# Expert weights loaded, waited for and freed by halves in a two-layer diffusion trunk

## What is computed

```python
g_p, g_i = lax.top_k(g_prob, 1)                    # one of 4 groups
e_p, e_i = lax.top_k(softmax(e_logits), TOP_K)     # two of its 4 experts
a = jnp.einsum('td,edf->tef', t, w_gate)           # w_gate, w_up: 16 x 1024 x 512
u = jnp.einsum('td,edf->tef', t, w_up)
hid = jax.nn.silu(a) * u * gates[..., None]
y = jnp.einsum('tef,efd->td', hid, w_down)         # w_down: 16 x 512 x 1024
```

## Time and profile before

| | us |
|---|---|
| median of three runs | 1182.11 (1179.56 to 1182.42) |
| the profiled execution | 1183.99 |
| its span, first to last instruction | 1182.1 |
| TensorE busy in the span | 1107.5 (94%) |
| VectorE, ScalarE, GpSimd busy | 388.3, 235.5, 93.2 |
| chain that ended last: TensorE, DMA, VectorE | 81%, 12%, 4% |

### The profile page before, as it was taken

How to read it: one execution, slowest core, us unless ns; L and a number is a source line. 1 busy time by engine, 2 the same in 40 slices (tenths; PEclk the granted TensorE clock), 3 DMA queues, 4 the chain that set the end, 5 groups by cost and what they waited for, 6 DMA issues and landing times.

```text
span 1182.1 us, 13463 instructions
## 1 busy us (share of the span) xinstructions
PE 1107.5 (94%) x5106; PEld 533.4 (45%) x5106; DVE 388.3 (33%) x982; ACT 235.5 (20%) x521; POOL 93.2 (8%) x160
## 2 busy tenths in 40 slices
PE   5999999999999899979999989999999899889998
PEld 1455545456456633323333434455656433333334
DVE  5223143443553611111111355553746211111113
ACT  2411201433224200000000232234544000000001
POOL 0000201010100101100010110000000001001010
PEclk9999999999999899999999989999999899999999
DMA  9843836351938949999959733322039999999964
GB/s 363 337 179 142 312 123 294 142 228 67 363 145 354 367 154 428 425 428 423 400 220 425 307 138 106 117 80 81 1 138 428 376 414 427 426 407 429 425 267 153
DMA packets 33126, 326.21 MB, mean 276 GB/s; under 512 B 6157, under 2 KB 7565, under 8 KB 15152
## 3 DMA queue, kind: packets, MB, share of 16 engines
q1 hardware_dynamic: 22176, 295.94, 60.7%
q0 software_dynamic: 10896, 29.52, 6.7%
HBM read 312.97 MB, written 22.28 MB: 284 GB/s over the span
## 4 chain that ended last, share of the span: by engine, by line
PE 81%; DMA 12%; DVE 4%; ACT 2%; issue 1%; SPq 0%; DVEq 0%; POOLq 0%; ACTq 0%
PE bank L1900 20%; PE bank L1822 14%; PE bank L1916 11%; PE bank L1814 9%; DMA arena<-in_moe 8%; PE bank L2110 7%; PE bank L1733 3%; PE bank L2032 2%; DMA h_rows<-hT 2%; PE bank L1858 1%; DMA ring<-in_proj 1%; PE bank L2077 1%; PE bank L1964 1%; PE bank L2094 1%; PE bank L2010 1%; PE bank L1926 1%
## 5 line engine op out<-in xcount | busy, mean ns | idle before, releaser
L1900 PE MATMUL bank<-arena,cT 128*64 128x512 f32 x880 | 237.4, 593 | 4.4 <-DMA arena<-in_moe 2.9
L1822 PE MATMUL bank<-ring,hT 128*128 128x512 f32 x384 | 171.0, 601 | 3.8 <-ACT hT L791 3.0
L1900 PE MATMUL bank<-ring,cT 128*64 128x512 f32 x464 | 151.4, 615 | 9.0 <-DMA ring<-in_moe 6.7
L1900 PEld LDWEIGHTS bank<-arena,cT 128*64 128x64 f32 x880 | 77.1, 137 | 121.8 <-issue 121.8
L1916 PE MATMUL bank<-arena,hT 128*64 128x512 f32 x512 | 116.3, 608 | 13.9 <-ACT hT L871 8.2
L1822 PEld LDWEIGHTS bank<-ring,hT 128*128 128x128 f32 x384 | 72.5, 193 | 90.3 <-issue 87.6
L1481 DVE TENSOR_TENSOR hT<-bank,hT 128x512 f32<-128x512 f32 x21 | 14.5, 691 | 288.2 <-PE bank L1900 288.2
L1814 PE MATMUL bank<-hT,ring 128*128 128x384 f32 x320 | 105.2, 487 | 0.0
L1900 PEld LDWEIGHTS bank<-ring,cT 128*64 128x64 f32 x464 | 48.5, 142 | 83.2 <-issue 83.2
L2110 PE MATMUL bank<-cT,ring 128*128 128x384 f32 x256 | 85.6, 491 | 0.0
L1814 PEld LDWEIGHTS bank<-hT,ring 128*128 128x128 f32 x320 | 60.3, 190 | 43.6 <-issue 3.9
(11 more groups left out here) (311 smaller groups left out, 1125.0 us busy)
## 6 DMA issues: line engine op xcount, KB each, us to landing
arena<-in_moe SPq DMA_DIRECT2D x66, 2048.0 KB, 20.3
ring<-in_proj SPq DMA_DIRECT2D x41, 2048.0 KB, 9.5
ring<-in_moe SPq DMA_DIRECT2D x30, 2048.0 KB, 18.5
y_rows<-cT POOLq DMA_DIRECT2D x12, 512.0 KB, 8.0
arena<-y_rows POOLq DMA_DIRECT2D x12, 512.0 KB, 6.2
h_rows<-hT POOLq DMA_DIRECT2D x6, 512.0 KB, 16.8
arena<-in_hyconst SPq DMA_DIRECT2D x1, 1792.0 KB, 11.9
xT<-in_x SPq DMA_DIRECT2D x1, 1536.0 KB, 8.1
```

Of the source, the lines that this page charges most:

```text
L1822: ins = mm(ps[:, :], src[:, k, P * i : P * i + P], w[:, k, :], start=k == 0, stop=k == KD - 1)
L1900: ins = mm(psum[kind][rows, :], mo["hS"][:, k, rows], w[side].rearrange("p (k n) -> p k n", k=KD)[:, k, :], start=k == 0, stop=k == KD - 1)
```

## The change

Each expert load becomes two transfers of 1 MB, one for each half of the slot's columns. The first half goes on as before with the semaphore `slot_loaded`, the second has one of its own, `rest_loaded`. For gate and up the halves are the steps k = 0 to 3 and k = 4 to 7. The down weights are laid out on the host so that their halves are the two halves of the output columns, which is the order in which TensorE uses them. TensorE waits for the second halves only when it comes to them, and tells by new semaphores (`gate_half`, `up_half`, `down_half`) that it is through with the first halves. SP issues a load's first half when the first half of the load nine places earlier is free, and its second half when that whole load is.

```diff
-                        consumed(layer, b - SLOTS)
-                    sp.dma_start(slot(s), moe_d[layer * MOE_LOADS + b // 6 * 6 + b % 2 * 3 + b % 6 // 2]).then_inc(slot_loaded[s], 16)
+                        consumed(layer, b - SLOTS, 0)
+                    half_slot = KD * HALF // 2
+                    src = moe_d[layer * MOE_LOADS + b // 6 * 6 + b % 2 * 3 + b % 6 // 2]
+                    sp.dma_start(slot(s)[:, 0:half_slot], src[:, 0:half_slot]).then_inc(slot_loaded[s], 16)
+                    if b >= SLOTS:
+                        consumed(layer, b - SLOTS, 1)
+                    sp.dma_start(slot(s)[:, half_slot:], src[:, half_slot:]).then_inc(rest_loaded[s], 16)
...
-                if kind == 0:
+                if half == 0:
+                    sp.wait_ge(sems[("gate_half", "up_half", "down_half")[kind]], end)
+                elif kind == 0:
                     sp.wait_ge(sems["gate_full"], end)
...
-                        for kind, done in ((0, "gate_full"), (1, "up_full")):
-
-                            w = weights(pair, kind)
+                        for kind, begun, done in ((0, "gate_half", "gate_full"), (1, "up_half", "up_full")):
+
                             for k in range(KD):
+                                if k % 4 == 0:
+                                    w = weights(pair, kind, k // 4)
...
+                                if k == 3:
+                                    ins.then_inc(sems[begun], 1)
...
-                        w = weights(pair, 2)
                         for half in range(2):
+                            w = weights(pair, 2, half)
                             pe.wait_ge(sems[f"y{half}_ready"], g)
                             for f in range(NF):
                                 for side in range(2):
                                     rows = slice(CAP * side, CAP * side + CAP)
-                                    wd = w[side].rearrange("p (f n) -> p f n", f=NF)
-                                    ins = mm(psum[DOWN_BANK + half][rows, :], mo["hidT"][:, f, rows], wd[:, f, HALF * half : HALF * half + HALF],
+                                    wd = w[side].rearrange("p (h f n) -> p h f n", h=2, f=NF)
+                                    ins = mm(psum[DOWN_BANK + half][rows, :], mo["hidT"][:, f, rows], wd[:, half, f, :],
                                              start=f == 0, stop=f == NF - 1)
+                                    if half == 1 and f == side == 0:
+                                        ins.then_inc(sems["down_half"], 1)
...
-    moe[:, :, 2] = a["moe_w_down"].reshape(DEPTH, NE, NF, P, D).transpose(0, 1, 3, 2, 4).reshape(DEPTH, NE, P, -1)
+    moe[:, :, 2] = a["moe_w_down"].reshape(DEPTH, NE, NF, P, 2, HALF).transpose(0, 1, 3, 4, 2, 5).reshape(DEPTH, NE, P, -1)
```

More of the change, by code:

```diff
@@ L394, in trunk_kernel @@
         slot_loaded = [sem(f"slot_loaded{s}") for s in range(SLOTS)]
+        rest_loaded = [sem(f"rest_loaded{s}") for s in range(SLOTS)]
         bank_full = [sem(f"bank_full{b}") for b in range(BANKS)]
@@ L414, in trunk_kernel @@
             sem("route_max"), sem("route_exp"), sem("assigned"), sem("slots_known"), sem("table_ready"), sem("idx_ready"))
-        loop_names = ("idx_copied", "to_copied", "gathered", "rows_full", "hS_ready", "gate_full", "up_full", "sg_ready", "hid_ready", "hidT_full",
+        loop_names = ("gate_half", "up_half", "down_half", "idx_copied", "to_copied", "gathered", "rows_full", "hS_ready", "gate_full", "up_full", "sg_ready", "hid_ready", "hidT_full",
                       "hidT_ready", "down_full", "y0_ready", "y1_ready", "rows_stored", "back0", "back1", "back2")
@@ L541, in moe_load, with moe_rest @@
             return s, earlier + moe_uses(layer, s).index(b) + 1
+        def moe_rest(layer, b):
+            s = moe_slot(layer, b)
+            return (len(moe_uses(0, s)) if layer else 0) + moe_uses(layer, s).index(b) + 1
         def slot(s):
@@ L615, in load_experts, with consumed @@
                             sp.wait_ge(table_ready, layer + 1)
-                        consumed(layer, b - SLOTS)
-                    sp.dma_start(slot(s), moe_d[layer * MOE_LOADS + b // 6 * 6 + b % 2 * 3 + b % 6 // 2]).then_inc(slot_loaded[s], 16)
+                        consumed(layer, b - SLOTS, 0)
[5 more added lines that the diff above has]
+                    sp.dma_start(slot(s)[:, half_slot:], src[:, half_slot:]).then_inc(rest_loaded[s], 16)
             pair_ends = {}
-            def consumed(layer, b):
+            def consumed(layer, b, half):
                 pair, kind, sems = b // 6, b % 6 // 2, loops[layer]
@@ L637, in _ @@
                 sp.wait_ge(loops[0][f"back{i}"], 32)
-            load_blocks(LAYER_BLOCKS[0], LAYER_BLOCKS[1], lambda s: consumed(0, moe_uses(0, s)[-1]))
+            load_blocks(LAYER_BLOCKS[0], LAYER_BLOCKS[1], lambda s: consumed(0, moe_uses(0, s)[-1], 1))
             load_experts(1)
@@ L1860, in rows_in, with weights @@
                             ins.then_inc(sems["rows_full"], 1)
[L1862 to L1867, removed]
+                def weights(pair, kind, half):
+                    loads = [6 * pair + 2 * kind + side for side in range(2)]
+                    for b in loads:
+                        s, load = moe_load(layer, b)
+                        if half == 0:
+                            pe.wait_ge(slot_loaded[s], 16 * load)
+                        else:
+                            pe.wait_ge(rest_loaded[s], 16 * moe_rest(layer, b))
+                    return [slot(moe_slot(layer, b)) for b in loads]
                 pe.wait_ge(table_ready, layer + 1)
```

## The result

The changed kernel takes 1172.96 us (median of four runs, 1171.77 to 1173.16) against 1181.66 us for the kernel before (four runs, 1179.56 to 1182.42). The ratio is 0.9931, with a 95% interval of 0.9917 to 0.9944: 8.7 us less, where the forecast from 1182.11 was 6.5 less, 1175.6. The profiled execution took 1171.77 us, with a span of 1169.9 us.

A forecast was written before the change was run, and what follows sets the result against it. TensorE work held 81% of the chain, with load 29's landing before down setting each layer's end. Halves, packets and the closed hole summed to -3.4 and -3.15 us, -6.5 from 1182.11: 1175.6 us, range 1171.5 to 1181.0.

The forecast's parts named there:

- Release by halves: Layer 0: load 9's first half issued 3.43 us earlier, putting the queue 2.45 us ahead up to load 29; layer 1: nothing.
- Waiting by halves: Down of pair 4, both layers: starting on first halves of loads 28 and 29 saves the last quarter, 2.45 us each.
- the earlier stops shrink by the same terms: Layer 0: TensorE's stops of 2.93, 3.36 and 0.40 us before down of pair 4 shrink by what the halves save.
- The stores and the hole: Layer 1: token-row stores take 11.3 us instead of 18.6, so load 8 issues earlier and a 2.8 us queue hole closes.
- Packets: 8 KB packets cost 0.07 us per load: 1.5 us over 21 loads in layer 0, 2.1 over 30 in layer 1.
- the line: Straight line through DMA packet times, 160 ns for 4 KB and 615 for 16 KB, giving 312 for 8 KB.
- The sum: Layer 0 -3.4 us and layer 1 -3.15 us, together -6.5 us, so 1175.6 us.
- The sign asked for: Load 29's last landing 0.9 us earlier in layer 0, about 0.7 in layer 1, counted from each layer's first tile.
- Packets cost nothing: Rival: smaller load packets have no price, so -10.1 us, 1172.0; chance 0.12.
- The hole stays: Rival: layer 1's queue hole remains, through another order of turns or load 8 held otherwise; -3.7 us, 1178.4; chance 0.16.
- Dead time per transfer: Rival: each of 51 added transfers costs 0.65 us unhidden in the full queue; +33 - 10.1, so 1205; chance 0.10.
- The clock takes it back: Rival: a lower-clock stretch falls on down with no load behind it, 2.8 us in each layer; 1181.2; chance 0.12.

The follow-up runs named there:

- e4: Kernel before with each load in two transfers, slots freed by halves, TensorE waiting for whole loads: 1178.24 us, ratio 0.9992.
- e2: Kernel before with each load in two transfers of 1 MB, waited for and freed whole: 1177.77 us, ratio 0.9981.
- e3: Kernel before with each load in two transfers, TensorE waiting by halves, slots freed whole: 1175.77 us, ratio 0.9961.
- e7: Kernel before without SP's wait for the stored token rows ahead of load 8, loads whole: 1179.38 us, ratio 0.9991.
- e1: Kernel before run and profiled again with no edit: 1179.07 us, ratio 1.0002 to the kernel before.
- e5: Changed kernel run and profiled again with no edit: 1172.22 us, ratio 0.9925 to the kernel before.

## Why the forecast came out

**Release by halves: right.** SP in order of time in the changed kernel (start us, us): the first two halves of load 9.

```profile
428.42 0.34 SPq L625 DMA_DIRECT2D arena<-in_moe  x1
431.85 0.33 SPq L628 DMA_DIRECT2D arena<-in_moe  x1
```

The first megabyte goes 3.43 us ahead of the second, as worked out. e4 less e2 gives 2.6 us in layer 0 for the 2.45, and nothing in layer 1 for the nothing.

**Waiting by halves: right.** 2.5 and 2.3 us by e3 less e2. In layer 0 of the changed kernel down starts at 541.10, when the first half of load 29 is there, while its second half lands at 543.3, behind the first matmuls of down. One remark of the forecast did not come out: that the earlier stops shrink by the same terms. The stop of 2.93 us is gone, but those ahead of gate and up of pair 4 are 3.15 and 3.36 us where they were 3.36 and 0.40; gate between them took 7.09 us instead of 9.91, so TensorE was there earlier and waited for the same queue.

**The stores and the hole: right in cause, the hole in size too.** The third store landed after 13.4 us where 11.3 were forecast, a miss of 2.1. It did no harm, since load 8 was issued 6.0 us before load 7 had landed. Layer 1 of the changed kernel where the hole was, and up to load 29:

```profile
913.00:921.00 8.00, 8.00 (x40) 2.82 (x38) 2.58 (x9) 0.60 (x1) 1.09 (x1) 1.00 1.02 419
921.00:1033.00 112.00, 100.21 (x470) 37.26 (x467) 13.96 (x22) 4.78 (x8) 9.69 (x16) 0.97 1.01 420
```

No hole. Load 8 lands 5.4 us behind load 7 instead of 8.1, and load 9 comes 2.3 us earlier in all, which with 0.55 us lost up to load 7 is 2.85 for the 2.8. Of the two things that the faster stores bring, an earlier load 8 and an earlier first tile, e7 has the first without the second, and there nothing was gained. That what TensorE gains at the gather is waited for again at load 29 held: before, it stopped 2.9 us for the first gathered rows of layer 1; after, it doesn't stop there, and still starts down 0.25 or 1.1 us behind the landing of load 29's first half.

**Packets: the mis-sized term.** The packets themselves came out as the line said, 312 ns for 8 KB, but "layer 1 pays it on 30, 2.1 us" was too much. It lost 0.55 us up to load 7, and from load 9 to load 29 it took 106.35 us against 105.78, 0.03 a load; 1.1 in all. With the second profiles (e1 and e5) in place of one or both of the first it is 1.3 to 1.7. The kernel before had already been slower in that stretch of layer 1 than in layer 0, 421 GB/s against 426, and the changed one runs at 420 in it. I took the rate of weights alone for the rate of that stretch; what made it lower is not shown. In layer 0 the term held: 1.24 us over 20 loads for 1.4 (1.84 against e1).

**The sum.** By stages layer 0 is 4.2 us shorter than the mean of the two profiles of the unchanged kernel, 265.36 (3.7 than the first; forecast 3.4). Layer 1 is 3.3 us shorter than their mean, 292.39, in one profile of the changed kernel and 4.2 in the other (forecast 3.15; with packets at 1.1, 4.15). That the first profile is so near to 3.15 is luck: the packets cost about 1 us less than forecast, and the clock took about 1 us back. The sign asked for, an earlier last landing of load 29, is 1.3 us in layer 0 (forecast 0.9) and 1.7 in layer 1 (forecast 0.7), there counted from the issue of load 0. Together the stages give 7.4 and 8.4 us; timed 8.7 and 8.6. What is left between, up to 1.3 us, is within the interval of the ratio, 1.6 us to each side; its cause is not shown.

**The rivals.** *Packets cost nothing* fell: they cost about what the line says in layer 0, half to four fifths of it in layer 1, and in quarters so much that the kernel is 6.2 us slower than with whole loads. *The hole stays* fell by the windows above. *Dead time per transfer* fell by 420 and 409 GB/s. *The clock takes it back* came true in small. Two windows of the changed kernel in gate and up of pair 4, layer 1 (the granted clock is third from the end):

```profile
1013.50:1017.00 3.50, 3.50 (x12) 1.12 (x10) 0.00 (x0) 0.00 (x0) 0.00 (x0) 0.53 1.01 419
1023.50:1027.50 4.00, 4.00 (x12) 1.38 (x10) 0.00 (x0) 0.00 (x0) 0.00 (x0) 0.57 1.02 424
```

Both stretches follow stops of TensorE for a load, 3.52 and 1.96 us (idle us and what ended it in brackets):

```profile
1012.55 8.78 PE L1918 MATMUL bank<-ring,cT 128*64 128x512 f32 x32 [3.52 <-DMA ring<-in_moe]
1023.30 0.61 PE L1918 MATMUL bank<-ring,cT 128*64 128x512 f32 x1 [1.96 <-DMA arena<-in_moe]
```

Gate's slow stretch vanished behind the next load. Up took 8.78 us, so down started at 1034.23, 1.1 us after the first half of load 29 had landed at 1033.10. In the second profile of the same kernel (e5) up was not slowed, down waited for the load, and the stage was 1.0 us shorter:

```profile
1003.40 28.26 DMA arena<-in_moe
...
1031.90 7.09 PE bank L1936 x32
```

So the clock took back 1 us in layer 1 of one of the two profiled executions, not 2.8 in each layer: the cover of a late load is thinner than before, but not gone.

## What to carry to other kernels

Where a load ended a stretch of the chain, cutting it into halves in the order of use paid at the wait (2.5 and 2.3 us), and at the release where a late release had left the queue empty (2.6 us, in layer 0 alone); the two gains added, since the queue stayed full between them. When two loads are needed together, put both first halves ahead of both second halves. And a stream of large packets set the pace of the other queue on the same engines: smaller packets made its stores faster (18.6 to 13.4 us) for 0.06 to 0.09 us a load, but cut once more they cost more than they gave.

## What the runs showed of the hardware that I had not expected

**Transfers of 64 partitions ran at half the rate**, 207 GB/s at a share of 0.93, with packets twice as long (1.24 us for 16 KB).

**SP stops when many transfers are outstanding.** Before, an issue took 0.67 us at most; after, up to 6.30. The ninth half of layer 1 and the one before it, in order of time (start us, us):

```profile
870.47 0.53 SPq L628 DMA_DIRECT2D arena<-in_moe  x1
871.04 2.16 SPq L625 DMA_DIRECT2D arena<-in_moe  x1
```

Eight halves go out in 0.4 to 0.5 us each, and from the ninth on the next four take about 2.1 us each, close to the time of a megabyte in the queue. In quarters, too, most issues in the full queue take about 1.1 us. Of the changed kernel's 48 load issues over 0.9 us, 45 began with ten or more of SP's earlier transfers not yet landed; before, an issue never met more than seven. That looks like a bound on the number of transfers under way, which no run here measured by itself. The DMA engines lose nothing by it here (a share of 1.01 from 921 to 1033), but SP can do nothing else while it stands in such an issue.
